# A two-layer hybrid RWKV/attention trunk on one core: the mixed-projection stage and the key-rate stage in one block, with key-rate block products inside a gate tile

## The chip, the cores and the metric

The kernel runs on one core of one Trainium2 chip. The metric is the device time of one execution in microseconds (us). PE is the matrix engine (TensorE), PEld its weight loads, DVE the vector engine, ACT the scalar engine, POOL the general-purpose engine (GpSimd), SP the engine that here only issues transfers. A wait in the profile is an engine's idle time with the instruction that ended it.

## The reference, cut to what matters

Two layers of a decoder trunk. Each layer multiplies the normalised residual stream h (1024 tokens and 16 meta tokens, 1024 channels) by one wide input matrix, whose columns feed an RWKV group, a latent-attention group and two gates:

```python
for l in range(DEPTH):
    p = h @ w_in[l]
    p_rwkv, p_mla, p_gate = jnp.split(p, [RWKV_COLS, RWKV_COLS + MLA_COLS], axis=-1)
    y_rwkv = _rwkv7_mix(p_rwkv, mu_shift[l], w0[l], w_lora_up[l], a0[l], a_lora_up[l], ...)
    y_mla = _mla(p_mla, pos, q_norm_g[l], w_uq[l], kv_norm_g[l], w_uk[l], w_uv[l])
    gate_rwkv, gate_mla = jnp.split(jax.nn.sigmoid(p_gate), N_BRANCHES, axis=-1)
    mixed = gate_rwkv * (y_rwkv @ w_proj_rwkv[l]) + gate_mla * (y_mla @ w_proj_mla[l])
    h = _layer_norm(DEEPNORM_ALPHA * h + mixed @ w_out[l], ln1_g[l], ln1_b[l])
    f = _conv_ffn(h, w_up[l], conv_w[l], conv_b[l], w_down[l])
    h = _layer_norm(DEEPNORM_ALPHA * h + f, ln2_g[l], ln2_b[l])
```

Inside `_rwkv7_mix` each column of p_rwkv is mixed with that of the token before (`p + (shift(p) - p) * mu`) and split into r, k, v and the low-rank inputs of decay and rate:

```python
w_raw = -jax.nn.softplus(-(w0 + jnp.tanh(wd) @ w_lora_up)) - 0.5
decay = jnp.exp(-jnp.exp(w_raw))
a = jax.nn.sigmoid(a0 + ad @ a_lora_up)
kk = kk / jnp.maximum(jnp.sqrt(jnp.sum(kk * kk, axis=-1, keepdims=True)), 1e-12)
k = k * (1.0 + (a - 1.0) * k_a)
```

The recurrence over tokens is computed in chunks of 104 tokens, for which the kernel prepares, per pair of heads, scaled copies of key, rate and query and the products of key and rate within each chunk.

## The kernel before, in words

Every stage is a `Phase`: one block with its own semaphores, which all engines leave through a barrier that also clears those semaphores. The change concerns two stages that follow each other in each of the two layers.

**The mixed-projection stage** (line 1433 on) forms 12 column tiles of 128 for r, k and v. A tile is `product` (line 226): for each of 8 slices k of the contraction, three passes (high by high, high by low, low by high halves of the fp32 numbers) of three 348-column matmuls, 72 in all, into one of two sets of three PSUM banks (`pset`). SP loads a 512 KB weight unit per tile, POOL splits it into its halves (lines 280 and 282), ACT copies the tile out (`raw0`/`raw1`, line 1551), DVE mixes neighbouring tokens (lines 1563 and 1565), ACT sends the result to HBM. Between its splits POOL forms sums of down-projection weights for a later stage (lines 1494 to 1500), with SP loading and storing them. At the end PE multiplies the first decay and rate products (`product32`, line 264, into both bank sets), then some matmuls that no one reads (`keep_warm`, line 257). SP has by then loaded the first mixed r, k, v and two units of gate weights, the first of which POOL splits (lines 287 and 289).

**The key-rate stage** (line 1638 on) works over four pairs of heads (j) and forms the 16 gate tiles G0 to G15 beside them. In the order of PE a pair is:

```python
pes.did(product32(one, [...]), f"zw{j}")          # decay, then za: rate; before j = 0 the stage before did both
pes.did(product32(one, [(head_ones[:, :], sqn[:, :])]), f"ss{j}")   # sums of squares
gate(g, two, ...); gate(g + 1, one, ...)          # two gate tiles
blocks(j, 0)                                      # key by rate, chunks 0 to 3
pes.did(product32(two, [(head_ones[:, :], rk[:, :])]), f"bn{j}")
blocks(j, 1)                                      # chunks 4 to 7
gate(g + 2, one, ...)
blocks(j, 2)                                      # chunks 8 and 9
```

`blocks` (line 1742) writes banks 6 and 7, and each part waits until ACT has copied the part before out of them (line 1799). For a pair ACT takes the sigmoids of decay and rate (lines 1814 and 1817), a logarithm and exponentials, the high halves of gate weights (`hi`, line 1782) and the gates' sigmoids (line 1788), after each of which it issues the store; DVE makes a running sum (line 1906), a maximum (line 1910), the low halves of gate weights (`lo`, line 1870) and the scaled copies up to `beta`, and beside the next pair it inverts 26 by 26 blocks of the pair before (lines 1876 and 1879). SP sends the copied-out blocks to HBM and back in the layout of that inversion (`pairs_out`, `blocks_in`), stores the inverses (line 1691) and loads weights. After the last pair, four gate tiles G12 to G15 remain, beside which the last inversion runs. The order on each engine is written out by hand as lists of step names; waits refer to these names.

An earlier stage already has a product with other matmuls within it: the hook `between` at line 1310 puts row sums (line 1288) ahead of slice k = 2 of a tile.

Of the kernel before, what the change touches and what calls it, by code (L numbers as in the profile page):

```python
# [18 lines left out]
ALU = mybir.AluOpType  # L19
# [134 lines left out]
def build(nc, a, out):  # L154
# [440 lines left out]
    def layer(l):  # L595
# [837 lines left out]
        with Phase(nc, "raw0_loaded", "raw1_loaded", "hi_done", "split", "used", "act_pre", "dve_pre",  # L1433
                   "act_steps", "dve_steps", "out0", "next_in",
                   "lora_in", "first0_in", "first1_in", "first_hi", "first_lo", "lora_up",
                   "wsum0_in", "wsum1_in", "wsum0_out", "wsum1_out", "wsum_steps") as (block, sm):
            loaded, hi_done, split, used = stream(sm[0:5])
            apre, dpre = Steps(sm[5], pre_act), Steps(sm[6], pre_dve)
            acts, dves = Steps(sm[7], ["raw0", "raw1"]), Steps(sm[8], ["mu0", "d0", "m0", "mu1", "d1", "m1"])
            outs = [Count(o, 1, 16) for o in (sm[9], rkv_landed[l])]  # L1440
            next_in = sm[10]
            lora_in, first_in, first_hi, first_lo, lora_up = sm[11], sm[12:14], sm[14], sm[15], sm[16]
            nt = 3 * RT
            wsum_in, wsum_out = sm[17:19], sm[19:21]
            sums = Steps(sm[21], [f"{n}{k}" for k in range(KF) for n in ("s1_", "s3_", "s2_", "s4_")])
            w_dn = a["w_down"][l]

            @block.sync
            def _(sp):
                def wsum_load(k):  # L1450
                    b = k % 2
                    if k >= 2:
                        sp.wait_ge(wsum_out[b], 16 * (k // 2))
                    for q, (kb, mb) in enumerate(((0, 1), (0, 0), (1, 1), (1, 0))):
                        sp.dma_start(wsum[b][:, q, :], w_dn[(kb * KF + k) * P:(kb * KF + k + 1) * P, mb * MF * P:(mb + 1) * MF * P]).then_inc(wsum_in[b], 16)

                def wsum_store(k):
                    sp.wait_ge(sums.sem, sums.of(0, f"s4_{k}"))
                    sp.dma_start(wsum_d[:, :, :, k, :].rearrange("q j p n -> p (q j) n"),
                                 wsum[k % 2][:, :, :].rearrange("p q (j n) -> p (q j) n", n=P)).then_inc(wsum_out[k % 2], 16)  # L1460
                split.give(sp)
                sp.sem_inc(split.sem, 2)
                for u in range(nt):
                    load_unit(sp, u + 2, u % 2, loaded, split, [(kview(KD), w_in_v[:, :, u * P:(u + 1) * P])])
                    if u in (0, 1):
                        wsum_load(u)
                    elif u >= 2:
                        wsum_store(u - 2)
                        if u < KF:
                            wsum_load(u)  # L1470
                wsum_store(KF - 1)
                sp.wait_ge(y_landed[l], 16 * (RT * NG // 2))
                sp.dma_start(w_l[0:DECAY_LORA, :], a["w_lora_up"][l, :, 0:P]).then_inc(lora_in, 16)
                sp.dma_start(w_l[DECAY_LORA:P, :], a["a_lora_up"][l, :, 0:P]).then_inc(lora_in, 16)
                sp.dma_start(reset[:, :], a["c_reset"]).then_inc(next_in, 16)
                sp.wait_ge(outs[0].sem, outs[0].of(RT + 1))
                for n in (1, 0, 2):
                    sp.dma_start(rkv[:, n, :], rkv_d[n * RT]).then_inc(next_in, 16)
                for s in range(2):
                    sp.wait_ge(split.sem, split.of(nt + s + 1))  # L1480
                    sp.dma_start(kview(KD)(w_raw[s]), w_in_v[:, :, GATE0 + s * P:GATE0 + (s + 1) * P]).then_inc(first_in[s], 16)
                sp.wait_ge(first_in[1], 16)
                for b in range(2):
                    sp.wait_ge(wsum_out[b], 16 * ((KF + 1 - b) // 2))
                sp.wait_ge(next_in, 16 * 4)

            @block.gpsimd
            def _(pool):
                def weight_sums(k):

                    b = k % 2
                    a11, a21, a12, a22 = (wsum[b][:, q, :] for q in range(4))
                    pool.wait_ge(wsum_in[b], 64 * (k // 2 + 1))
                    sums.did(nc.gpsimd.tensor_tensor(a22, a21, a22, ALU.add), f"s1_{k}")
                    pool.wait_ge(sums.sem, sums.of(0, f"s1_{k}"))
                    sums.did(nc.gpsimd.tensor_tensor(a21, a11, a21, ALU.subtract), f"s3_{k}")
                    pool.wait_ge(sums.sem, sums.of(0, f"s3_{k}"))
                    sums.did(nc.gpsimd.tensor_tensor(a11, a22, a11, ALU.subtract), f"s2_{k}")
                    pool.wait_ge(sums.sem, sums.of(0, f"s2_{k}"))
                    sums.did(nc.gpsimd.tensor_tensor(a12, a12, a11, ALU.subtract), f"s4_{k}")  # L1500
                used.give(pool)
                sums.give(pool)
                pool.sem_inc(hi_done.sem, 2)
                for u in range(nt):
                    split_unit(pool, u + 2, u % 2, u // 2 + 1, loaded, hi_done, split, (used.sem, used.of(u + 1)))
                    if u < KF:
                        weight_sums(u)
                pool.wait_ge(first_in[0], 16)
                pool.wait_ge(used.sem, used.of(nt + 1))
                split_next(pool, 0, first_hi, first_lo)  # L1510

            @block.tensor
            def _(pe):
                def tile(u, s):
                    pe.wait_ge(split.sem, split.of(u + 1))
                    product(pset[s], KD, wtile(w_hi[s], KD), wtile(w_lo[s], KD), hk(h_hi), hk(h_lo)).then_inc(used.sem, 1)
                pe.sem_inc(used.sem, 1)
                tile(1, 1)
                with pe.Fori(0, nt // 2) as i:
                    for s in range(2):  # L1520
                        pe.wait_ge(apre.sem, apre.of(0, ("raw_a", "raw_b")[s]))
                        pe.wait_ge(acts.sem, acts.of(i, f"raw{s}", 1))
                        tile(i * 2 + (2 + s), s)
                pe.wait_ge(lora_in, 32)
                pe.wait_ge(apre.sem, apre.of(0, "tanh"))
                for s in range(2):
                    rows = slice(s * DECAY_LORA, P if s else DECAY_LORA)
                    pe.wait_ge(acts.sem, acts.of(nt // 2 - 1, f"raw{s}"))
                    product32(pset[s], [(w_l[rows, :], lora_x[rows, :])]).then_inc(lora_up, 1)
                keep_warm(7, 3)  # L1530
                pe.wait_ge(lora_up, 2)

            @block.scalar
            def _(act):
                apre.give(act)
                acts.give(act)
                for s in range(2):
                    outs[s].give(act)
                for s in range(2):
                    act.wait_ge(used.sem, used.of(s + 1))  # L1540
                    act.wait_ge(dpre.sem, dpre.of(0, "pad1"))
                    apre.did(nc.scalar.activation(chunks3(raw_p[s][:, 1:TP + 1]), pset[s], ACT.Copy), ("raw_a", "raw_b")[s])
                act.wait_ge(dpre.sem, dpre.of(0, "m_c"))
                apre.did(nc.scalar.activation(lora_x[0:DECAY_LORA, :], lora_x[0:DECAY_LORA, :], ACT.Tanh), "tanh")
                apre.did(nc.scalar.activation(gd0[:, :], gd0[:, :], ACT.Sigmoid), "sg0")
                apre.did(nc.scalar.activation(gd1[ROPE:ROPE + G1, 1:TP + 1], gd1[ROPE:ROPE + G1, 1:TP + 1], ACT.Sigmoid), "sg1")
                with act.Fori(0, nt // 2) as i:
                    for s in range(2):
                        act.wait_ge(used.sem, used.of(i * 2 + (3 + s)))
                        act.wait_ge(dves.sem, dves.of(i, f"m{s}", 1))  # L1550
                        acts.did(nc.scalar.activation(chunks3(raw_p[s][:, 1:TP + 1]), pset[s], ACT.Copy), f"raw{s}")  # L1551
                        act.wait_ge(dves.sem, dves.of(i, f"m{s}"))
                        act.dma_start(rkv_d[i * 2 + s], mixed_p[s][:, :]).then_inc(outs[s].sem, 16)
# [28 lines left out]

        cursor[0] = gate_end
# [2443 lines left out]
```

## Time and profile before, and how to read it

| | us |
|---|---|
| three timed executions | 3688.88, 3690.66, 3691.11 |
| their median | 3690.66 |
| profiled execution, first to last instruction (span) | 3684.4 |
| PE busy in it | 3527.1 |
| DVE, POOL, ACT busy in it | 2374.1, 1538.0, 1316.6 |

For the profiled execution only its span is given, with no device time of its own; the median of the timed runs lies 6.26 us above the span. In the rows below a timeline line gives start and length in us, then engine, source line, operation, tiles written and read, the number of instructions merged, and in brackets the idle time before them with what ended it. "PEclk" is the granted clock of TensorE as a share of full speed.

### The profile page before, as it was taken

How to read it: one execution, taken by the hardware profiler on the slowest of the kernel's cores; microseconds unless marked ns; L12 is line 12 of the kernel's file. 1: busy time of each engine (PE TensorE's matmuls, PEld its weight loads, DVE VectorE, ACT ScalarE, POOL GpSimd, SP SyncE). 2: the span in 40 equal slices, each digit the busy share in tenths (PEclk: the TensorE clock that was granted, in tenths of full speed). 3: DMA queues.
4: the chain of work that ended last, by engine and by line, in shares of the span. 5: the costliest groups of instructions: out<-in, count | busy, mean ns of one | idle time of the engine just before them, and what ended most of it. 6: DMA issues, size and time to landing. Idle time of an engine off the chain costs nothing. (4 is left out here: it accounts for less than half of the span.)

```text
span 3684.4 us, 69094 instructions
## 1 busy us (share of the span) xinstructions
PE 3527.1 (96%) x29239; PEld 3297.9 (90%) x29239; DVE 2374.1 (64%) x2821; ACT 1316.6 (36%) x1900; POOL 1538.0 (42%) x875
## 2 busy tenths in 40 slices
PE   6999999999999999999999999999999999999998
PEld 6867988988898999999987689888889989999998
DVE  2374447665658877777835643585657597777687
ACT  5343124212213444453443520441231144444435
POOL 5364930000742655544444569000026435555341
PEclk9999999999999999999999999999999999999999
DMA  5521866422522222273334248563234122222732
GB/s 121 146 64 53 251 204 187 143 72 58 169 75 76 75 81 76 82 266 121 86 69 136 59 128 260 177 191 100 77 114 130 36 92 81 82 80 81 264 119 85
DMA packets 476187, 439.00 MB, mean 119 GB/s; under 512 B 106027, under 2 KB 401159, under 8 KB 475895
## 3 DMA queue, kind: packets, MB, share of 16 engines
q1 hardware_dynamic: 455640, 383.02, 34.5%
q10 hardware_dynamic: 20255, 51.78, 3.8%
q8 instruction: 221, 3.62, 0.4%
q14 instruction: 71, 0.58, 0.0%
HBM read 297.14 MB, written 137.05 MB: 118 GB/s over the span
## 5 line engine op out<-in xcount | busy, mean ns | idle before, releaser
L234 PE MATMUL psum<-h_hi,w_hi 128*128 128x348 f32 x1632 | 355.3, 326 | 10.7 <-ACT lat_sq L864 3.7
L234 PE MATMUL psum<-h_lo,w_hi 128*128 128x348 f32 x1632 | 348.7, 322 | 0.0
L234 PE MATMUL psum<-h_hi,w_lo 128*128 128x348 f32 x1632 | 347.6, 321 | 0.0
L234 PEld LDWEIGHTS psum<-h_hi,w_hi 128*128 128x128 f32 x1632 | 274.7, 189 | 19.6 <-POOL w_lo L282 4.3
L234 PEld LDWEIGHTS psum<-h_lo,w_hi 128*128 128x128 f32 x1632 | 277.3, 189 | 0.0
L234 PEld LDWEIGHTS psum<-h_hi,w_lo 128*128 128x128 f32 x1632 | 274.9, 188 | 0.0
L3255 POOL TENSOR_TENSOR piece_lo_w<-sum,piece_hi_w 128x512 fp32r<-128x512 f32 x120 | 209.5, 1746 | 141.6 <-ACT piece_hi_w L3557 138.5
L3300 PE MATMUL psum<-t_hi,piece_hi_w 128*128 128x260 f32 x1280 | 258.2, 283 | 5.1 <-issue 2.6
L3300 PE MATMUL psum<-t_hi,piece_lo_w 128*128 128x260 f32 x1280 | 257.3, 282 | 0.0
L3300 PE MATMUL psum<-t_lo,piece_hi_w 128*128 128x260 f32 x1280 | 257.2, 282 | 0.0
L280 POOL TENSOR_TENSOR w_hi<-w_raw,consts 128x1024 fp32r<-128x1024 f32 (+1 forms) x78 | 126.9, 1627 | 295.5 <-PE psum L234 108.8
L2032 POOL TENSOR_TENSOR g<-gd,g_hi 32x1044 fp32r<-32x1044 f32 x2 | 4.8, 2390 | 535.3 <-ACT g_hi L2210 535.3
L3300 PEld LDWEIGHTS psum<-t_hi,piece_hi_w 128*128 128x128 f32 x1280 | 197.7, 188 | 6.3 <-DVE t_lo L3843 3.3
L3300 PE MATMUL psum<-h_hi,piece_hi_w 128*128 128x260 f32 x960 | 194.0, 283 | 6.3 <-DVE uv_second L3879 5.3
L3300 PEld LDWEIGHTS psum<-t_lo,piece_hi_w 128*128 128x128 f32 x1280 | 197.4, 188 | 0.0
L3300 PEld LDWEIGHTS psum<-t_hi,piece_lo_w 128*128 128x128 f32 x1280 | 196.7, 188 | 0.0
L3300 PE MATMUL psum<-h_hi,piece_lo_w 128*128 128x260 f32 x960 | 194.1, 283 | 0.0
L3300 PE MATMUL psum<-h_lo,piece_hi_w 128*128 128x260 f32 x960 | 193.7, 283 | 0.0
L3255 POOL TENSOR_TENSOR piece_lo_w<-raw_g,piece_hi_w 128x512 fp32r<-128x512 f32 x80 | 123.8, 1547 | 157.3 <-ACT piece_hi_w L3557 157.3
L282 POOL TENSOR_TENSOR w_lo<-w_raw,w_hi 128x1024 fp32r<-128x1024 f32 (+1 forms) x78 | 175.6, 2251 | 6.1
L1563 DVE TENSOR_TENSOR diff<-raw_p 128x1044 f32<-128x1044 f32 x28 | 52.4, 1871 | 184.7 <-ACT raw_p L1551 164.6
L3807 DVE SCALAR_TENSOR_TENSOR cg_row<-ug_row,vecs,cg_row 128x1040 f32<-128x1040 f32 x80 | 130.7, 1634 | 50.6 <-ACT cg_row L3503 50.6
(655 smaller groups left out, 9749.7 us busy)
## 6 DMA issues: line engine op xcount, KB each, us to landing
w_raw<-in_w_in SPq DMA_DIRECT2D x68, 512.0 KB, 8.8
wsum<-in_w_down SPq DMA_DIRECT2D x88, 256.0 KB
wsum_scratch<-wsum SPq DMA_DIRECT2D x22, 1024.0 KB
raw_g<-in_w_up SPq DMA_DIRECT2D x40, 512.0 KB, 3.8
raw_v<-in_w_up SPq DMA_DIRECT2D x40, 512.0 KB, 3.9
gate_scratch<-gst ACTq DMA_DIRECT2D x32, 522.0 KB, 3.0
gbuf<-gate_scratch SPq DMA_DIRECT2D x32, 522.0 KB, 3.6
prep_scratch<-prep ACTq DMA_DIRECT2D x8, 2080.0 KB, 8.3
```

Of the source, the lines that this page charges most:

```text
L234: last = nc.tensor.matmul(bank[:, n, :], w(k), x(k)[:, nrange(n)], start=(k == 0 and q == 0), stop=(k == kt - 1 and q == 2))
L280: nc.gpsimd.tensor_tensor(w_hi[s][:, 0:width], w_raw[s][:, 0:width], consts[:, 4:5].broadcast_to([P, width]), ALU.mult).then_inc(hi_done.s ...
L282: nc.gpsimd.tensor_tensor(w_lo[s][:, 0:width], w_raw[s][:, 0:width], w_hi[s][:, 0:width], ALU.subtract).then_inc(split.sem, 1)
L1563: me.did(nc.vector.tensor_tensor(d[rows, :], raw[rows, 0:TP], raw[rows, 1:TP + 1], ALU.subtract), names[0])
L2032: nc.gpsimd.tensor_tensor(g96[G1R, 1:TP + 1], gd1[G1R, 1:TP + 1], g0_hi[G1R, :], ALU.subtract).then_inc(gate_low, 1)
L3255: w_los.did(nc.gpsimd.tensor_tensor(piece_lo_w[:, q, :], weight_piece[q], piece_hi_w[:, q, :], ALU.subtract), f"{q}_{p}")
L3300: last = nc.tensor.matmul(psum[:, bank + c, 0:TQ], w, x_(k)[:, c * TQ:(c + 1) * TQ], start=(not more and k == 0 and n == 0), stop=(k == MF ...
L3807: dves.did(stt(c, t[:, n:T + n], vecs[:, at + 2 * n * FT:at + 2 * n * FT + 1], c, ALU.mult, ALU.add), f"t{n}{x_}{p}")
```

## The change

The two stages become one block: one set of semaphores, and no barrier between them. The first gate weights are loaded and split as a thirteenth unit of the first stage, so that G0 follows the last r, k, v tile directly. The first decay product, sum of squares and rate product are put into G0 ahead of slices 1, 3 and 5. So each pair now has the gate tiles g + 1, g + 2 and g + 3 in place of g, g + 1 and g + 2, and three tiles (G13 to G15) remain after the last pair. Parts two and three of a pair's blocks are put into tile g + 3, ahead of its slices 2 and 5. The other engines' orders follow: ACT and DVE take the first pair's steps in the order in which G0 needs them, loads and splits of gate weights come one unit earlier, and ACT copies the third part of the blocks out before the sigmoid of the tile that now holds it. The `keep_warm` matmuls between the stages go. The diff, cut to its core (moved code left out):

```diff
-        with Phase(nc, "raw0_loaded", "raw1_loaded", "hi_done", "split", "used", "act_pre", "dve_pre",
-                   "act_steps", "dve_steps", "out0", "next_in",
...
+        with Phase(nc, "raw0_loaded", "raw1_loaded", "hi_done", "split", "used", "act_pre", "dve_pre",
+                   "r_act_steps", "r_dve_steps", "out0", "lora_in",
...
             @block.sync
...
+                load_unit(sp, nt + 2, 0, loaded, split, [(kview(KD), w_in_v[:, :, GATE0:GATE0 + P])])
+                wsum_store(KF - 1)
...
+                for u in (1, 2):
+                    sp.wait_ge(split.sem, split.of(nt + 1 + u))
+                    sp.dma_start(kview(KD)(w_raw[u % 2]), w_in_v[:, :, GATE0 + u * P:GATE0 + (u + 1) * P]).then_inc(raw_in[u % 2].sem, 16)
...
             @block.gpsimd
...
-                split_next(pool, 0, first_hi, first_lo)
+                split_unit(pool, nt + 2, 0, nt // 2 + 1, loaded, hi_done, split, (used.sem, used.of(nt + 1)))
...
             @block.tensor
...
-                keep_warm(7, 3)
-                pe.wait_ge(lora_up, 2)
...
+                def first_rows(k):
+                    if k == 1:
+                        pe.wait_ge(lora_in, 32)
+                        pe.wait_ge(apre.sem, apre.of(0, "tanh"))
+                        pe.wait_ge(racts.sem, racts.of(nt // 2 - 1, "raw1"))
+                        pes.did(product32(pset[1], [(w_l[0:DECAY_LORA, :], lora_x[0:DECAY_LORA, :])]), "zw0")
+                    if k == 3:
+                        pe.wait_ge(acts.sem, acts.of(0, "sq0"))
+                        pes.did(product32(pset[1], [(head_ones[:, :], sqn[:, :])]), "ss0")
+                    if k == 5:
+                        pe.wait_ge(dves.sem, dves.of(0, "ssm0"))
+                        pes.did(product32(pset[1], [(w_l[DECAY_LORA:P, :], lora_x[DECAY_LORA:P, :])]), "za0")
+                pe.wait_ge(split.sem, split.of(nt + 3))
+                pe.wait_ge(racts.sem, racts.of(nt // 2 - 1, "raw0"))
+                pes.did(product(pset[0], KD, wtile(w_hi[0], KD), wtile(w_lo[0], KD), hk(h_hi), hk(h_lo), first_rows), "G0")
...
-                    gate(g, two, (acts.sem, acts.of(0, f"a{j}")))
-                    gate(g + 1, one, (dves.sem, dves.of(0, f"ssm{j}")))
+                    gate(g + 1, two, (acts.sem, acts.of(0, f"a{j}")))
+                    gate(g + 2, one, (dves.sem, dves.of(0, f"ssm{j}")) if j else (acts.sem, acts.of(0, "g0")))
                     blocks(j, 0)
-                    pe.wait_ge(acts.sem, acts.of(0, f"g{g}"))
+                    pe.wait_ge(acts.sem, acts.of(0, f"g{g + 1}"))
                     pe.wait_ge(dves.sem, dves.of(0, f"rk{j}"))
                     pes.did(product32(two, [(head_ones[:, :], rk[:, :])]), f"bn{j}")
-                    blocks(j, 1)
-                    gate(g + 2, one, (acts.sem, acts.of(0, f"g{g + 1}")))
-                    blocks(j, 2)
+                    def later_blocks(k, j=j):
+                        if k in (2, 5):
+                            blocks(j, 1 if k == 2 else 2)
+                    gate(g + 3, one, (acts.sem, acts.of(0, f"g{g + 2}")), later_blocks)
...
             @block.scalar
...
-                square(0)
+                hi(1)
...
+                    act.wait_ge(pes.sem, pes.of(0, f"zw{j}"))
+                    acts.did(nc.scalar.activation(chunks3(sw[:, :]), one if j else two, ACT.Sigmoid, bias=vcol(V_W0, j)), f"sw{j}")
+                    if j == 0:
+                        mixed_out(nt // 2 - 1, 1)
+                        square(0)
+                        wsum_landed(act)
+                        hi(2)
...
                     if j + 1 < RT:
                         square(j + 1)
-                    gate(g + 2, one)
                     blocks(j, 2)
+                    gate(g + 3, one)
...
             @block.vector
...
+                lo(1)
                 dve.wait_ge(reset_in, 16)
                 dve.wait_ge(mid_pad, 1)
+                dve.wait_ge(rdves.sem, rdves.of(nt // 2 - 1, "m1"))
...
+                    if j == 0:
+                        lo(2)
                     dve.wait_ge(pes.sem, pes.of(0, f"ss{j}"))
...
-                    lo(g + 2)
                     lo(g + 3)
+                    lo(g + 4)
```

Between the sigmoid of zw0 and the square, ACT issues the store of the last mixed tile (`mixed_out`), which waits for DVE's `m1` of that tile; `wsum_landed` waits for the last store of the weight sums, whose memory later tiles reuse.

## Rows read from the trace of the kernel before

**Rows 1.** The page, busy time of the engines over the whole span.
```profile
PE 3527.1 (96%) x29239; PEld 3297.9 (90%) x29239; DVE 2374.1 (64%) x2821; ACT 1316.6 (36%) x1900; POOL 1538.0 (42%) x875
```

**Rows 2.** Waits of PE over the whole span: us in total, times, longest.
```profile
PE psum L264 <- ACT sw L1814: 12.5, 8, 5.8
...
PE psum L1742 <- ACT adg L1799: 6.9, 8, 1.6
```

**Rows 3.** Timeline of PE where the two stages meet, layer 0.
```profile
504.78 3.30 PE L264 MATMUL psum<-lora_x,w_l 64*128 64x348 f32 x12
...
516.20 3.85 PE L264 MATMUL psum<-sqn,head_ones 128*128 128x348 f32 x6 [5.84 <-ACT sw L1814]
519.33 1.59 PE L234 MATMUL psum<-h_hi,w_hi 128*128 128x348 f32 x3
...
521.45 0.64 PE L234 MATMUL psum<-h_hi,w_lo 128*128 128x348 f32 x3
```

**Rows 4.** Windows, same place: us, busy of PE, PEld, DVE, ACT, POOL, PEclk, DMA.
```profile
516.20:519.33 3.13, 3.13 (x7) 1.92 (x7) 2.50 (x2) 2.25 (x2) 0.00 (x0) 0.50 0.45 134
```

**Rows 5.** Timeline of PE where the two stages meet, layer 1.
```profile
2312.89 3.30 PE L264 MATMUL psum<-lora_x,w_l 64*128 64x348 f32 x12
...
2325.34 1.58 PE L234 MATMUL psum<-h_hi,w_hi 128*128 128x348 f32 x3
...
2327.30 0.64 PE L234 MATMUL psum<-h_hi,w_lo 128*128 128x348 f32 x3
```

**Rows 6.** Timeline of ACT, sigmoid of the last gate tile of layer 0.
```profile
740.63 1.04 ACT L1788 ACTIVATE gst<-psum 128x1044 f32<-128x1044 f32 x1 [10.41 <-PE psum L234]
```

**Rows 7.** Timeline of PE, row sums inside a product, an earlier stage.
```profile
341.97 0.63 PE L234 MATMUL psum<-h_hi,w_lo 128*128 128x348 f32 x3
342.53 0.68 PE L1288 MATMUL psum<-racc,ones 128*64 128x272 f32 x4
...
343.73 0.63 PE L234 MATMUL psum<-h_lo,w_hi 128*128 128x348 f32 x3
```

**Rows 8.** Timeline of PE around one pair of heads, layer 0.
```profile
559.62 0.61 PE L1742 MATMUL psum<-prep 64*104 64x104 f32 x8
560.07 2.77 PE L264 MATMUL psum<-lora_x,w_l 64*128 64x348 f32 x12
563.23 2.02 PE L264 MATMUL psum<-sqn,head_ones 128*128 128x348 f32 x6 [0.39 <-ACT sw L1814]
564.83 0.90 PE L234 MATMUL psum<-h_hi,w_hi 128*128 128x348 f32 x3
565.56 0.64 PE L234 MATMUL psum<-h_lo,w_hi 128*128 128x348 f32 x3
...
588.99 2.02 PE L264 MATMUL psum<-rk,head_ones 128*128 128x348 f32 x6
592.21 0.98 PE L1742 MATMUL psum<-prep 64*104 64x104 f32 x16 [1.20 <-ACT adg L1799]
593.12 0.74 PE L234 MATMUL psum<-h_hi,w_hi 128*128 128x348 f32 x3
```

**Rows 9.** Timeline of ACT, POOL and DVE where the stages meet, layer 0.
```profile
505.91 1.89 POOL L287 TENSOR_TENSOR w_hi<-w_raw,consts 128x1024 fp32r<-128x1024 f32 x1 [12.82 <-DMA w_raw<-in_w_in]
...
508.94 3.27 DVE L1565 SCALAR_TENSOR_TENSOR mixed_p<-diff,mu,raw_p 128x1044 f32<-128x1044 f32 x1
...
515.03 1.11 ACT L1814 ACTIVATE sw<-psum,vecs 128x1044 f32<-128x1044 f32 x1
...
516.28 2.33 DVE L1906 TENSOR_TENSOR_SCAN cum<-reset,sw 128x1040 f32<-128x1040 f32 x1 [2.25 <-ACT sw L1814]
...
520.08 1.25 DVE L1910 TENSOR_SCALAR sqn<-psum 128x1044 f32<-128x1044 f32 x1 [1.27 <-PE psum L264]
```

**Rows 10.** Timeline of SP and PE at the end of the key-rate stage, layer 0.
```profile
728.45 3.02 SPq L1691 DMA_DIRECT2D inverse_scratch<-tit  x4
...
740.43 1.56 PE L257 MATMUL psum<-pair_mask,ident 104*104 104x416 f32 x4
```

More of the change, by code:

```diff
@@ L1638, in layer @@
-        dve_n += [f"lo{g + 2}"] + solve_names(RT - 1, 0) + [f"lo{g + 3}"] + solve_names(RT - 1, 1)
-        with Phase(nc, "raw0_loaded", "raw1_loaded", "pe_steps", "act_steps", "dve_steps",
+            pe_n += [f"zw{j}", f"za{j}", f"ss{j}"] if j else ["zw0", "ss0", "za0", "G0"]
+            pe_n += [f"G{g + 1}", f"G{g + 2}", f"P{j}_0", f"bn{j}", f"P{j}_1", f"P{j}_2", f"G{g + 3}"]
+            act_n += [f"sw{j}", f"a{j}"] if j else ["hi1", "sw0", "sq0", "hi2", "a0"]
+            act_n += [f"ln{j}", f"rn{j}"] + [f"{n}{j}" for n in ("eA", "eR", "eB", "eK", "eD")] + ([] if j else ["g0"])
@@ new lines, in layer @@
+            lora_in = sm[10]
+            nt = 3 * RT
+            wsum_in, wsum_out = sm[11:13], sm[13:15]
+            sums = Steps(sm[15], [f"{n}{k}" for k in range(KF) for n in ("s1_", "s3_", "s2_", "s4_")])
+            w_dn = a["w_down"][l]
+            raw_in = [Count(s, 0, 16) for s in sm[16:18]]
+            pes, acts, dves = Steps(sm[18], pe_n), Steps(sm[19], act_n), Steps(sm[20], dve_n)
+            rkv_in, w_got, reset_in = sm[21:24]
+            bonus_out, prep_out = Count(sm[24], 0, 16), Count(sm[25], 0, 16)
@@ L1723, in _, with tile @@
             @block.tensor
             def _(pe):
-                pes.give(pe)
-                def gate(u, bank, free):
-                    if u >= 1:
-                        pe.wait_ge(dves.sem, dves.of(0, f"lo{u}"))
+                def tile(u, s):
+                    pe.wait_ge(split.sem, split.of(u + 1))
+                    product(pset[s], KD, wtile(w_hi[s], KD), wtile(w_lo[s], KD), hk(h_hi), hk(h_lo)).then_inc(used.sem, 1)
+                pe.sem_inc(used.sem, 1)
+                tile(1, 1)
@@ new lines, in _ @@
+                with pe.Fori(0, nt // 2) as i:
+                    for s in range(2):
+                        pe.wait_ge(apre.sem, apre.of(0, ("raw_a", "raw_b")[s]))
+                        pe.wait_ge(racts.sem, racts.of(i, f"raw{s}", 1))
+                        tile(i * 2 + (2 + s), s)
+                pes.give(pe)
+                def first_rows(k):
[10 more added lines that the diff above has]
+                        pes.did(product32(pset[1], [(w_l[DECAY_LORA:P, :], lora_x[DECAY_LORA:P, :])]), "za0")
@@ L1832, in _ @@
                     acts.did(nc.scalar.activation(decay[:, j, :], dsum[:, :], ACT.Exp, scale=-DECAY_C), f"eD{j}")
-                    hi(g + 2)
-                    gate(g, two)
+                    if j == 0:
+                        gate(0, one)
                     hi(g + 3)
+                    gate(g + 1, two)
+                    hi(g + 4)
                     act.wait_ge(dves.sem, dves.of(0, f"beta{j}"))
@@ L1838, in _ @@
                                   prep[:, :, :, :].rearrange("p c q n -> p c (q n)")).then_inc(prep_out.sem, 16)
-                    gate(g + 1, one)
-                    hi(g + 4)
+                    gate(g + 2, one)
+                    hi(g + 5)
                     blocks(j, 0)
```

333 lines of the change are left out of this document (143 added, 190 removed).

## The prediction

> **What bounds the kernel now.** I read the page first: PE is busy for 96% of the span and no other engine for two thirds of it [rows 1], so a change pays only where PE waits, runs slowly or does useless work. The list of waits names the two places that the change touches: PE before the sums of squares, waiting for ACT's decay sigmoid (8 times, 12.5 us, one of them 5.8), and PE before the key-rate blocks, waiting for ACT to empty their banks (8 times, 6.9 us) [rows 2]. Then the timeline where the stages meet. In layer 0 the last r, k, v tile ends at 504.78, where the first decay and rate products start; then come the matmuls that no one reads, 5.84 us of nothing, the sums of squares at 516.20 and G0 at 519.33 [rows 3]. The granted clock, 1.00 while the tiles run, is 0.50 in that last stretch, the lower level of 1.2 GHz [rows 4]: the sums of squares take 3.85 us where a later pair takes 2.02 [rows 3, 8], and the first two passes of G0 take 2.12 us (519.33 to 521.45). In layer 1 the same stretch goes from 2312.89 to 2325.34 and 2327.30 [rows 5].
>
> **Units.** ACT waits 10.41 and works 1.04 between two gate tiles at the end of the stage, so a tile with nothing in it takes 11.45 us [rows 6]: 1.43 for each of its 8 slices, 0.477 for each of its 24 passes. What putting something into a tile costs is seen in an earlier stage: without the row sums the pass at 343.73 would start two passes after 341.97, at 342.92. The insertion cost 0.81 us for 0.68 us of matmuls, so 0.13 beyond its own busy time [rows 7]. I take 0.13 for each insertion, from the only place where this kernel does it. The bounds are 0 and, since what follows a sum of squares also starts with a slow pass (0.73 in place of 0.477, [rows 8]), 0.38.
>
> **Part 1, the meeting of the stages.** Before, from the end of the last tile to the end of G0: 504.78 to 521.45, then 22 passes of 0.477, so 27.2 us in layer 0, and by the same sum 24.9 in layer 1. That is 52.1 in all. After: one tile (11.45), both decay and rate products (2.77), the sums of squares (2.02 at full clock) and three insertions (0.39): 16.6 us a layer, if nothing waits. The gap of 5.84 goes, and with it the reason for the lower clock, since PE never stops.
>
> Does anything wait? I count from the end of the last tile. PE is through slice 0 at 1.43; ACT has emptied the tile's banks at about 1.25 (the 1.04 of such a pass and its start), so zw0 can go: PE until 2.95. ACT meanwhile makes the high halves of unit 1 (to 2.3), takes the sigmoid (2.95 to 4.1, 1.11 in [rows 9]), issues the store of the last mixed tile (DVE's two passes at 1.25 each are done by about 3.9), then squares (to about 5.6). PE is through slices 1 and 2 at 5.8: the sums of squares wait for nothing, or for a tenth or two. They end at 7.95. DVE: low halves of unit 1 to 5.1, running sum 2.33 to 7.5, low halves of unit 2 to 8.7, maximum 1.25 to 10.0 [rows 9]; PE wants it at slice 5, at 10.8. The rest is looser: G2 needs G0's sigmoid, behind a logarithm and exponentials on ACT, some 3 us before PE asks.
>
> What lies ahead of this chain on other queues: unit 1 of the gate weights must be in SBUF at 1.25. Before, the first gate unit, issued at the same point of SP's queue, had landed when POOL took it up at 505.91, that is at 1.13 [rows 9]. SP issues one unit more before the weight sums' last store, but one less later, so the transfers in that queue are the same; POOL splits the extra unit right after tile 12, a whole tile (11.45) ahead of G0, and its first half takes 1.89 [rows 9]. The DVE pass that took 3.27 us while POOL was splitting [rows 9] should be back at 1.25, since POOL has nothing left then. I allow 0.3 us of waiting per layer: 16.9 after, so 52.1 - 33.8 = **18.3 us** saved in both layers.
>
> **Part 2, the blocks inside the third tile.** Before, around one pair: from the sums bn (588.99) to the tile after part two (593.12) 4.13 us, with 1.20 of waiting, 0.10 for that tile's slow first pass (0.74 where 0.64 is usual), and 0.45 for part three ahead of zw (559.62 to 560.07): 4.68. After: from bn to the tile directly, as from the sums of squares to theirs (563.23 to 564.83, 1.60, and 0.25 of slow first pass), part two 0.98 + 0.13, part three 0.61 + 0.13: 3.70 [rows 8]. So 0.98 is saved where 1.20 was waited, 0.22 less than the wait. The 8 waits average 0.86 [rows 2]: 8 x 0.64 = **5.1 us**. ACT has 2 slices (2.9 us) after bn to empty the banks, of which it needs some 1.2, then three slices more, so no new wait stands there. Between 0 (insertions at the upper bound use it up) and 6.9.
>
> **What moves and costs nothing.** za of the next pair now waits for the sigmoid of the tile just finished, in the same banks. ACT needs 1.04 and PE spends half of 2.77 on zw meanwhile: covered by about 0.2 us, and if that cover fails, by tenths. ACT squares the next pair's keys ahead of emptying part three; the keys are asked for right after bn, and part three is multiplied five slices and part two later (8.2 us), so only a transfer of more than some 7 us would make that late, and ACT alone. SP sends the blocks out earlier. At the end of the stage three whole tiles and three slices follow the last part, in place of four tiles: 7.2 us less cover for the last inversion. Before, its last store was issued by 731.47, 9.0 us ahead of the last tile's end at 740.43 [rows 10]; ACT now empties part three without a sigmoid ahead of it (1.04), so some 2.8 remain for the landing. Just covered; past it, each microsecond is lost.
>
> **The sum.** 18.3 + 5.1 = 23.4 us. The traced span of 3684.4 is 6.26 below the median of the runs; what lies around the span is untouched, so I subtract from the median: 3690.66 - 23.4 = **3667.3 us**. A difference of under 0.2% (7.4 us) can't be told from none.
>
> **Rivals.**
>
> *The chain within G0 runs late.* DVE, ACT and a transfer must keep a pace that was hidden before by an idle PE; the margins are 0 to 0.8 us. For it: the unit in SBUF only 0.1 us ahead, and orders in which high halves stand ahead of the sigmoid. Against it: the same transfers had landed in time. Each microsecond late costs one per layer; late by 3 gives back 6: 3673. At worst the old wait of 5.84 returns twice: 3679.
>
> *The last inversion ends the stage.* If the stores land 5 us late in both layers, 10 are given back: 3677. For it the margin of 2.8; against it, nothing else is left in that queue.
>
> *The insertions break PE's pace: slower than before.* PE would lose its clock in tiles that hop between banks. Five tiles a layer hold insertions. At 1.2 GHz a tile takes 11.45 us more; with half of each of the ten tiles at that level 57 us are lost: 3725. It decides from 2.3 us a tile, 1.6 slices at the lower level. Against it: after the one insertion that I can see, passes go on at full pace, and tiles change bank with every matmul as it is; the clock fell only after 5.84 us of idleness.
> The Trainium skill, "TensorE: Matmul & The Clock Gate", section "A second HAM failure mode: psum-queue depth-cycling", speaks for this rival: cycling through PSUM banks can leave short idle gaps in which the clock gate swings between its levels, and throughput falls. By that rule the time would be this rival's; the trace so far does not agree, with 0.477 us a pass in tiles that cycle three banks.
>
> *The change does not do what it says.* If the meeting point merely moves the wait (G0's weights split late, say, because POOL is also busy with weight sums), little but part 2 is left: about 3686. POOL's last sums end one tile and more before; small.
>
> **How the numbers follow.** Forecast 0.68, around 3667 (3662 to 3671); late chain 0.14; inversion 0.07; no real effect 0.07; slower 0.04. The low end takes no waits in G0 (0.6) and insertions at 0 (22 x 0.13 = 2.9): 3663.8, or 3662 if part 2 gives all of its 6.9. The high end takes insertions at 0.38 (11 a layer, 5.5) and half of a late chain: 3677. Faster by over 0.2% needs 3683.3 or less: 0.68 + 0.14 + 0.07 less the worst of these two, 0.88. Within 0.2%: 0.08; slower: 0.04.
>
> **What would show it.** Right: G0's first pass within 0.2 us of the last tile's end; no idle of PE above a few tenths until the first pair's blocks; granted clock 1.00 throughout; the decay product after 3 passes, the sums of squares after 9; no wait of PE for the emptied banks in the list; part three 4.3 us ahead of the tile's end; the stage's barrier right after the last sigmoid. Wrong: PE idle ahead of the sums of squares or the rate product in G0, with ACT or a transfer as releaser; a wait of SP for inverse stores after the last tile; passes of tiles with insertions above 0.5 us.

## The result, and the profile after

Four executions of the changed kernel took 3656.03 to 3671.33 us, median 3660.07; four of the kernel before, 3690.89. The ratio is 0.992 [0.9901, 0.994]: faster by 0.8%, 30.8 us where 23.4 were forecast. The forecast ratio, 3667.3 / 3690.66 = 0.9937, lies within that interval, but the median of 3660.07 lies below the low end of the range, 3662.

The traced execution spans 3660.2 us, 24.2 less than that of before. PE's busy time is the same to 0.7 us [rows 1]; what went is time in which PE stood. Page, busy time of the engines:

```profile
PE 3526.4 (96%) x29227; PEld 3297.2 (90%) x29227; DVE 2374.8 (65%) x2821; ACT 1315.9 (36%) x1900; POOL 1539.3 (42%) x875
```

Waits of PE over the whole span (us in total, times, longest); both waits of [rows 2] are gone from the list, and the wait for POOL's halves, also in the list before, is now among the largest of this part of the program:

```profile
PE psum L528 <- DVE tok L434: 13.5, 1, 13.5
PE psum L1256 <- ACT q_hi L1331: 7.9, 18, 0.6
PE psum L264 <- ACT grs L3454: 5.5, 2, 2.9
...
PE psum L234 <- POOL w_lo L282: 3.8, 6, 1.5
```

Where the stages meet in layer 0 (timeline of PE; compare [rows 3]), G0's first pass at 501.77 follows the last tile without a gap. No row of the window has a bracket, so PE never stood:

```profile
501.77 0.65 PE L234 MATMUL psum<-h_hi,w_hi 128*128 128x348 f32 x3
...
503.30 2.02 PE L264 MATMUL psum<-lora_x,w_l 64*128 64x348 f32 x6
505.25 0.74 PE L234 MATMUL psum<-h_hi,w_hi 128*128 128x348 f32 x3
505.83 0.64 PE L234 MATMUL psum<-h_lo,w_hi 128*128 128x348 f32 x3
506.31 0.63 PE L234 MATMUL psum<-h_hi,w_lo 128*128 128x348 f32 x3
...
508.21 1.92 PE L264 MATMUL psum<-sqn,head_ones 128*128 128x348 f32 x6
509.70 0.90 PE L234 MATMUL psum<-h_hi,w_hi 128*128 128x348 f32 x3
...
512.35 0.64 PE L234 MATMUL psum<-h_hi,w_lo 128*128 128x348 f32 x3
512.92 2.02 PE L264 MATMUL psum<-lora_x,w_l 64*128 64x348 f32 x6
514.87 0.74 PE L234 MATMUL psum<-h_hi,w_hi 128*128 128x348 f32 x3
```

Windows of the same place, G0, then G1 with G2, then all from the last r, k, v tile to the next stage (us; busy of PE, PEld, DVE, ACT, POOL; PEclk; DMA share; GB/s). PE is busy throughout G0 to G2, and the granted clock is 1.00 in all three, where [rows 4] show 0.50:

```profile
501.77:519.34 17.57, 17.57 (x93) 14.71 (x92) 13.99 (x14) 9.55 (x9) 0.00 (x0) 1.00 0.37 107
519.34:542.24 22.90, 22.90 (x145) 22.68 (x144) 9.80 (x9) 10.99 (x12) 0.00 (x0) 1.00 0.46 166
501.77:728.10 226.33, 224.94 (x1414) 208.34 (x1413) 151.66 (x295) 95.80 (x108) 0.00 (x0) 1.00 0.53 166
```

Around a pair (timeline of PE; compare [rows 8]) parts two and three stand between passes of one tile:

```profile
547.96 0.98 PE L1684 MATMUL psum<-prep 64*104 64x104 f32 x16
548.87 0.74 PE L234 MATMUL psum<-h_hi,w_hi 128*128 128x348 f32 x3
...
553.35 0.61 PE L1684 MATMUL psum<-prep 64*104 64x104 f32 x8
553.89 0.73 PE L234 MATMUL psum<-h_hi,w_hi 128*128 128x348 f32 x3
...
558.37 3.22 PE L264 MATMUL psum<-lora_x,w_l 64*128 64x348 f32 x12
561.61 2.02 PE L264 MATMUL psum<-sqn,head_ones 128*128 128x348 f32 x6
```

End of the stage, timelines of SP and of PE (compare [rows 10]):

```profile
720.39 3.02 SPq L1587 DMA_DIRECT2D inverse_scratch<-tit  x4
728.03 8.44 SPq L2023 DMA_DIRECT2D xc<-inverse_scratch  x16
```

```profile
725.21 1.56 PE L257 MATMUL psum<-pair_mask,ident 104*104 104x416 f32 x4
728.10 0.60 PE L2074 MATMUL psum<-pc 64*104 64x208 f32 x4 [1.33 <-SPq L2010]
```

**Where the 24.2 us came from.** I cut each trace at four points: the end of the last r, k, v tile (504.78 before; 501.77 after) and the first product of the next stage (743.23; 728.10), in both layers. The two stretches in between hold everything the change touches. In the first layer the stretch went from 238.45 to 226.33, in the second from 236.74 to 226.33: 22.5 us. The other 1.7 lie in stages whose code is the same.

Each stretch splits at part one of pair 0 (543.49 before, 542.24 after, with G0, G1 and with G0, G1, G2 ahead of it) and at the end of the last tile:

| us saved | layer 0 | layer 1 | sum | forecast |
|---|---|---|---|---|
| meeting: to part one, less G1 or less G1 and G2 at 11.45 each | 27.26 - 17.57 = 9.7 | 24.97 - 17.57 = 7.4 | 17.1 | 18.3 |
| pairs: part one of pair 0 to the end of the last tile | 2.5 | 3.1 | 5.6 | 5.1 |
| end of the stage | -0.1 | -0.1 | -0.2 | 0 |

### The profile page after: what moved, and what is told of

Read it like the earlier page. It is cut to its first block and busy times, and to the rows that moved or that the text cites. A ratio compares the mean times of both kernels' runs of the same rounds, so it can differ in the third digit from the quotient of the medians.

```text
span 3660.2 us, 68992 instructions
## 1 busy us (share of the span) xinstructions
PE 3526.4 (96%) x29227; PEld 3297.2 (90%) x29227; DVE 2374.8 (65%) x2821; ACT 1315.9 (36%) x1900; POOL 1539.3 (42%) x875
```

## The experiments

Nine experiments ran, three of them repeats without an edit. "Stretch" is the one just defined; the rest is the span less both stretches. Clock is the mean granted clock over the timed runs, where the list of runs gives it.

| kernel | ratio to before | stretches, layers 0 and 1 | rest of the traced span | clock |
|---|---|---|---|---|
| before | | 238.45, 236.74 | 3209.2 | |
| before again | 0.9996 [0.9986, 1.0006] | 238.45, 237.60 | 3209.2 | 0.9888 (51 runs) |
| changed | 0.992 [0.9901, 0.994] | 226.33, 226.33 | 3207.5 | 0.9914 (16 runs, all three) |
| changed, again | 0.9926 [0.9909, 0.9944] | 226.38, 226.37 | 3211.9 | |
| changed, third | 0.9924 [0.991, 0.9939] | 226.38, 226.37 | 3214.2 | |
| merge only | 0.9954 [0.994, 0.9968] | 231.87, 231.17 | 3217.3 | 0.9898 |
| parts only | 0.9984 [0.9974, 0.9995] | 233.98, 234.21 | 3224.0 | 0.9881 |
| rows first | 0.9973 [0.9964, 0.9983] | 234.75, 234.95 | 3216.8 | 0.9887 |
| near parts | 0.9928 [0.9912, 0.9943] | 226.40, 226.39 | 3211.4 | 0.9912 |
| rows near | 0.9929 [0.9912, 0.9946] | 227.89, 227.88 | 3207.6 | 0.9915 |
| warm meeting | 1.0003 [0.9991, 1.0015] | 239.45, 240.92 | 3208.5 | 0.9903 |

The stretches are a sharper measure than the runs: in the three traces of the changed kernel they agree to 0.05 us, while the rest, which no edit touched, differs by 16.5 us over the eleven traces.

### The changed kernel again, and a third time

No edit.

> The changed kernel, nothing else altered. The two traces put 12.2 us (first layer) and 10.5 us (second) of the gain between the end of the last r,k,v tile and the end of the stage, 22.7 in all, while the medians of the timed runs stood 30.8 apart. Theory A (the stage gains what was forecast, and the other 7 to 8 us are differences between executions in stages that the change doesn't touch): in a new trace the two stretches take 223 to 224 us again, within 0.5, and the median of new runs lies anywhere from 22 to 31 below the kernel before. Theory B (the stage gains more in most executions than in the one traced): the two stretches come out 3 us or more shorter than 223.4, with the median again about 30 below.

> The changed kernel a third time. Two traces give 226.3 and 226.4 us for each of the four stretches from the end of the last r,k,v tile to the first product of the next stage, against 238.5 and 236.7 before: 22.5 us, within 0.1 in each trace. In the untouched rest the times differ by up to 17 us from execution to execution, with the stretches in which the clock stands at half. Theory A (22.5 in the stretches is the whole effect; the distance of the medians beyond it is the spread of the rest): stretches of 226.3 to 226.4 again, a median between 3660 and 3672, and at the same mean clock (0.990) an execution 20 to 23 us under one of the kernel before. Theory B (the change also makes the rest faster by 4 to 8 us, through fewer stretches at half clock elsewhere): again a mean clock of 0.991 to 0.993 over the runs where the kernel before has 0.988 to 0.989, and a median of 3664 or less.

Medians 3664.59 (3655.18 to 3670.08, 6 runs) and 3660.36 (3657.98 to 3668.64, 6 runs) against 3689.72 (22 runs) and 3690.34 (17 runs): 25.1 and 30.0 us. The stretches are the same as in the first trace, so the touched stages gain 22.5 and no more, and theory B of the first expectation fails. (The first expectation measures to the end of the last tile, 223.4; the stretch here goes 2.9 further, to the next stage's first product.) Of the two theories of the second expectation neither is excluded: the stretches, the median and the mean clock (0.9914 over all runs against 0.9888) fit both. Compared at the same mean clock, the distance is 20 us (0.990: median 3666.4 of 5 runs, against 3686.2 of 14) or 24 us (0.991: 3662.0 of 5, against 3685.9 of 4). So the touched stages gain what the traces show, and what the medians show beyond it goes with a higher clock over the run.

### The kernel before, again

No edit.

> The kernel before, for a second trace and its mean clock over the runs. The stretch from the last r,k,v tile to the next stage's first product comes out between 236 and 239 us in each layer (its meeting holds a stretch at half clock whose place may move by a microsecond or two). The time outside the span is 2.1 us as in every timed run, so that the execution traced first (span 3684.4) was one of about 3686.5 us, 4 us under the median of the runs. If instead 4 us or more lie outside the span of the traced execution, the distance between span and median was not a matter of which execution was traced.

Median 3688.2 (12 runs). The traced execution took 3687.31 with a span of 3685.2: 2.1 us lie outside the span. In the changed kernel it is 1.8 (3662.03 and 3660.2). Over all runs it is 1.7 to 1.9 in the kernels with one block and 2.1 to 2.2 in those with two. The execution traced first (span 3684.4) was therefore one of about 3686.5 us. Against this second trace the changed kernel's stretches save 23.4.

### Merge only

```diff
-                    gate(g + 3, one, (acts.sem, acts.of(0, f"g{g + 2}")), later_blocks)
+                    blocks(j, 1)
+                    gate(g + 3, one, (acts.sem, acts.of(0, f"g{g + 2}")))
+                    blocks(j, 2)
```

with ACT's order put back to match.

> One block and G0 with its three insertions as in the changed kernel; parts two and three of each pair stand outside the gate tile as in the kernel before. By the sum of the forecast (18.3 for the meeting, 5.1 for the pairs) this is 5.1 slower than the changed kernel: each stretch from the last r,k,v tile to the end of the stage takes 226.0 instead of 223.4, and the wait of part two on the eviction of part one is back at about 0.86 x8. Rival (the pairs gain nothing, since what the insertions cost eats the wait): same time as the changed kernel within 1 us. Rival (the meeting gains little by itself): 15 us or more slower than the changed kernel.

Each stretch is 5.5 and 4.8 us longer than in the changed kernel: 10.3, twice what was expected. Up to the end of the last tile 2.5 and 1.7 of it appear: these are the waits of the pairs, back in the list and about as forecast. The other 6 us come at the end of the stage. Waits of PE, the first row twice 4.4 where the changed kernel has 1.3:

```profile
PE psum L2073 <- SPq L2009: 8.8, 2, 4.4
...
PE psum L1684 <- ACT adg L1771: 5.4, 8, 1.2
...
PE psum L264 <- ACT sw L1785: 2.3, 6, 0.4
```

Timelines of SP and PE at that end:

```profile
730.17 3.32 SPq L1587 DMA_DIRECT2D inverse_scratch<-tit  x4
736.31 7.93 SPq L2022 DMA_DIRECT2D xc<-inverse_scratch  x16
```

```profile
730.44 1.56 PE L257 MATMUL psum<-pair_mask,ident 104*104 104x416 f32 x4
736.38 1.03 PE L2073 MATMUL psum<-pc 64*104 64x208 f32 x4 [4.38 <-SPq L2009]
```

The last inverse stores are issued by 733.49 and SP goes on 2.82 later: here the last inversion ends the stage. With part three of the last pair behind tile g + 3, and no longer with four tiles to come, the inversion starts too late. So the two parts of the change are not independent. Taking over a tile from the first pair shortens the cover of the last inversion, and moving part three into the tile gives most of it back.

### Parts only

The edit of merge only the other way round, on the kernel before: two blocks, with parts two and three ahead of slices 2 and 5 of tile g + 2.

> The kernel before with its two blocks, with parts two and three of each pair inside the third gate tile. By the sum of the forecast 5.1 us faster than the kernel before (each stage 2.5 shorter than the 233.9 to 235.7 before), the wait on the eviction of part one gone, the wait for the decay sigmoid (12.5 over 8) untouched. Rival (insertions eat the wait): within 1 us of the kernel before.

Ratio 0.9984 [0.9974, 0.9995], 3.7 us between the medians. From part one of pair 0 to the end of the last tile it takes 194.63 in both layers, where before took 196.94 and 197.53: 5.2 saved, against 5.1 expected. (The whole stretches differ by 7.0, because the meeting also varies from trace to trace: PE's wait there was 5.84 and 4.37 in the first trace, 5.17 and 4.62 in the second.) The wait on the emptied banks is gone. Of the 8 waits for the decay sigmoid two are left, those of the meeting; the expectation had called all 8 untouched. Waits of PE:

```profile
PE psum L264 <- ACT sw L1816: 9.3, 2, 4.8
```

### Rows first

```diff
-                pes.did(product(pset[0], ..., first_rows), "G0")
+                pes.did(product(pset[0], ...), "G0")
```

with the calls `first_rows(1)`, `(3)` and `(5)` ahead of G0.

> The changed kernel with the three small products of pair 0 (zw, ss, za) ahead of G0 in place of inside it: the block is still one, but PE stands through the chain. From the trace of the changed kernel: waits of about 1.5 (eviction of the last tile), 2.3 (decay sigmoid and square) and 1.9 (maximum) us, so 5.7 per layer less the three insertions' own overhead of about 0.35 each: 4.6 per layer, 9 us in all slower than the changed kernel, if hiding the chain inside G0 is worth what its waits show. If the clock falls over the chain as it did before the change (0.50 in one stretch), 1 to 3 us per layer more. If nearly all of the 18 us came from the barrier and the reload between the blocks and not from the chain, less than 3 us slower.

17.0 us are given back, not 9: 8.4 and 8.6 per layer. That leaves 5.5 of the 22.5, which is what parts two and three bring by themselves. One block without the chain inside G0 is worth nothing. Timeline of PE, then the window behind the second wait:

```profile
512.83 2.08 PE L264 MATMUL psum<-lora_x,w_l 64*128 64x348 f32 x6 [1.22 <-ACT raw_p L1739]
517.18 3.85 PE L264 MATMUL psum<-sqn,head_ones 128*128 128x348 f32 x6 [2.27 <-ACT sqn L1781]
522.37 2.02 PE L264 MATMUL psum<-lora_x,w_l 64*128 64x348 f32 x6 [1.34 <-DVE sqn L1914]
```

```profile
517.00:519.00 2.00, 1.82 (x3) 1.18 (x4) 1.97 (x3) 1.07 (x2) 0.00 (x0) 0.50 0.85 204
```

The brackets are 4.83 per layer, near the 5.7 expected. The rest is the clock: after the stands it is 0.50, and the sums of squares take 3.85 in place of 1.92.

### Near parts

```diff
-                        if k in (2, 5):
+                        if k in (2, 3):
```

> The changed kernel with part three of each pair one slice (1.43 us) after part two in place of three slices after it. The eviction of a part takes two activations of 0.66 us or so each and showed a wait of 0.6 to 1.6 us where 2.0 us of other work stood between. If the spacing is what removed that wait: a wait of 0.5 to 1.3 us is back at part three of each of 8 pairs, 4 to 10 us in all, so that each stage stretch grows from 226.3 to 228.5 to 231. If one slice is enough: within 0.3 us of 226.3, and the gain came from the insertion as such.

The stretches are 226.40 and 226.39, the same as in the changed kernel, so one slice is enough, and the expectation was wrong about the cause. Timeline of PE:

```profile
548.14 0.98 PE L1684 MATMUL psum<-prep 64*104 64x104 f32 x16
...
550.66 0.61 PE L1684 MATMUL psum<-prep 64*104 64x104 f32 x8
```

Between the two parts PE has 1.6 us of work, no more than the sums bn gave before, and yet no wait. The timeline of ACT in the kernel before, around part one (543.49), shows why it was different there:

```profile
543.60 1.04 ACT L1788 ACTIVATE gst<-psum 128x1044 f32<-128x1044 f32 x1 [8.87 <-PE psum L234]
...
545.15 1.06 ACT L1782 ACTIVATE w_hi<-w_raw 128x1024 fp32r<-128x1024 f32 x1 [0.51 <-DMA w_raw<-in_w_in]
546.11 0.91 ACT L1799 ACTIVATE adg<-psum 104x416 f32<-104x416 f32 x2
```

Copying a part out takes 0.91 us, but ACT first had the sigmoid of the tile just finished and a high half to do. The wait was for ACT's queue at a tile's end. In the middle of a tile that queue is empty.

Part of that queue is itself a wait, for the weights of a later gate tile: the bracket ahead of the high half. In the kernel before it is 0.46 or 0.47 where PE waits 0.60, and it is 0.47 in the changed kernel too, where the row names no transfer. Around the second pair of layer 0 it is longer, and PE's wait there, 1.20 [rows 8], is longer by the same 0.6 (timeline of ACT, kernel before):

```profile
590.29 1.06 ACT L1782 ACTIVATE w_hi<-w_raw 128x1024 fp32r<-128x1024 f32 x1 [1.07 <-DMA w_raw<-in_w_in]
```

So of the 6.9 us in eight waits, 4.8 (0.60 each) are the queue, and 2.1 are gate weights that had not landed.

### Rows near

```diff
-                    if k == 3:
+                    if k == 2:
...
-                    if k == 5:
+                    if k == 3:
```

> The changed kernel with the insertions of pair 0 ahead of slices 1, 2 and 3 of G0 in place of 1, 3 and 5. By the trace the squares are done 5.78 us and the maximum 9.74 us after the end of the last tile; ahead of slice 2 PE stands at 4.9 and ahead of slice 3 at about 8.9. So waits of 0.9 and 0.9 us are expected, 1.8 per layer and 3.6 in all, each stretch 228.1 in place of 226.3. If these short waits also bring the clock down in the stage, 1.5 to 3 us more per layer. If the chain is faster than the stamps say (no waits), 226.3.

Timeline of PE, layer 0:

```profile
511.06 2.02 PE L264 MATMUL psum<-sqn,head_ones 128*128 128x348 f32 x6 [0.65 <-ACT sqn L1779]
...
515.04 2.02 PE L264 MATMUL psum<-lora_x,w_l 64*128 64x348 f32 x6 [0.53 <-DVE sqn L1912]
```

Waits of 0.65 and 0.53 where 0.9 and 0.9 were expected, and stretches longer by 1.5. The chain runs at the pace the stamps showed, slices 3 and 5 give it what it needs, and waits as short as these did not bring the clock down.

### Warm meeting

On the kernel before, at the end of the r, k, v block:

```diff
-                keep_warm(7, 3)
+                keep_warm(7, 7)
```

> The kernel before with seven dummy products in place of three at the end of the r,k,v block (5.5 us in place of 2.3), so that PE stands 2.7 us in place of 5.8 (first layer) and 1.3 in place of 4.4 (second) at the meeting; nothing waits less. If the clock at the meeting falls because PE stands still there: the product ss of pair 0 runs at full clock (2.0 us in place of 3.85 and 3.2), the granted clock of the stretch behind it stays above 0.9, the two stage stretches shrink from 238.5 and 236.7 by 2 to 4 us each, and the mean clock of the runs rises by about 0.0014 over the 0.9888 of the kernel before. If the clock's fall has nothing to do with the length of the stand: 238 again. If clearing the meeting of half clock also spares half clock in stages behind it (what would explain 4 us by which the runs of the changed kernel gain more than the stretches): a mean clock of 0.991 or more, and a time 8 us or more under the kernel before.

Timeline of PE, layer 0, and the window behind it:

```profile
506.02 5.14 PE L257 MATMUL psum<-pair_mask,ident 104*104 104x416 f32 x14
514.36 3.62 PE L264 MATMUL psum<-sqn,head_ones 128*128 128x348 f32 x6 [3.21 <-ACT sw L1814]
```

```profile
515.00:520.00 5.00, 5.00 (x20) 3.76 (x19) 3.92 (x4) 2.31 (x3) 0.00 (x0) 0.70 0.14 40
```

It failed as a test of the clock: PE still stood for 3.21 us in both layers, where 2.7 and 1.3 were expected, and the clock still fell. The stretches are 1.0 and 4.2 longer. From the end of the last tile to part one of pair 0 both layers take 38.1 us, against 38.7 and 36.4 before, so the longer row of dummy products held up the meeting in the second layer alone. The rest lies behind it, with the waits on emptied banks, 4.8 us in each layer against 3.2 and 3.7, and in the second layer with a lower clock after the first of them (part two of pair 0 takes 1.64 us there in place of 0.98). In pair 0 of the first layer the gate weights landed late (timelines of ACT and PE):

```profile
544.06 1.06 ACT L1782 ACTIVATE w_hi<-w_raw 128x1024 fp32r<-128x1024 f32 x1 [2.01 <-DMA w_raw<-in_w_in]
545.98 0.98 PE L1742 MATMUL psum<-prep 64*104 64x104 f32 x16 [2.15 <-ACT adg L1799]
```

It does show a floor for this order: even when PE comes to the barrier late, it stands 3.2 us until ACT has squared and taken the sigmoid. Whether a meeting at full clock would make later stages faster stays open. The mean clock over the runs was 0.9903, against 0.9891 in the 17 runs of the kernel before beside them, and no time was gained.

## Why the prediction was right, and where it was wrong

**The direction and the places were right.** Waits for the emptied banks and for the decay sigmoid left the list, PE stands for no more than 0.1 us from the last r, k, v tile to the barrier at the end of the stage, the clock is 1.00 there, and part three ends 4.5 us ahead of its tile's end (4.3 forecast).

**Part 1: 17.1 against 18.3.** The before side was right (27.26 and 24.97, forecast 27.2 and 24.9). The after side is 17.57 per layer, forecast 16.9. Nothing waits, so the 0.3 allowed for that was not used; the insertions cost more. From the pass ahead of an insertion to the one behind, less a pass of 0.477, and with the slow first pass after it, zw0 and za0 take 2.1 each and ss0 1.8. The forecast had 1.39 + 0.13 for each of the first two and 2.02 + 0.13 for the third. The 1.39 was half of a pair of products that ran behind another small product [rows 8]; directly behind a tile the same pair takes 3.24 (558.37 to 561.61) in place of 2.77, and one of the two alone takes 1.95 to the next pass (503.30 to 505.25), more than half of either. That is the term of this part that was mis-sized. A row of the kernel before pointed to it: in [rows 3] the pair stands directly behind a tile, and takes 3.30.

The chain's times were right to a few tenths. Counted from the end of the last tile, the squares are done at 5.78 (forecast 5.6), the sums of squares end at 7.93 (7.95) and the maximum is done at 9.74 (10.0). PE asks for it at 11.15 (10.8).

**Part 2: 5.6 against 5.1,** 5.2 when done alone. The insertions cost 1.1 for part two and 0.7 for part three, as forecast (1.11 and 0.74). The reading of the wait was incomplete: it counted how long ACT needs to empty the banks, while most of it was ACT's queue ahead of that (near parts). And that the sum is met so closely is partly luck. It books 0.45 per pair for taking part three from ahead of zw, but the pair of products, now directly behind the tile, grew by 0.47; and the wait of 0.39 for the decay sigmoid, which the sum left alone, went away. The two nearly cancel in the six places where a pair follows.

**The last inversion** is "just covered", as forecast. Its last store was issued by 723.41, 1.8 us ahead of the last tile's end where 2.8 were forecast. The 2.82 us that merge only shows from the last store to SP's next transfer hold the landing and then the barrier. The barrier alone takes 1.26 in the changed kernel, from the end of PE's last dummy product at 726.77 to SP's next transfer at 728.03. So the landing takes some 1.6 us, an estimate, and is done at about 725.0, before those dummy products end. In merge only this rival came true and cost 3 us per layer.

**The late chain** did not happen; rows near prices it.

**The insertions do not break PE's pace.** Passes between insertions still follow at 0.477 (505.83, 506.31, 506.78) and the granted clock is 1.00 in tiles with insertions. The Trainium skill, "TensorE: Matmul & The Clock Gate", section "A second HAM failure mode: psum-queue depth-cycling", tells of a kernel that cycles through PSUM banks, in which PE idles briefly between groups of matmuls and the clock swings. The trace shows neither here, with no idle of PE and 1.00 over the 17.57 us of G0.

**What failed is the step from the sum to the time and its range: whatever lies outside the two stages was put at nothing.** Of the 30.8 us between the medians the stretches hold 22.5; the other 8.3 lie elsewhere. "The traced span of 3684.4 is 6.26 below the median of the runs; what lies around the span is untouched, so I subtract from the median." Only 2.1 us lie around the span (1.8 in the changed kernel, so this too is not quite untouched); the other 4.2 were the traced execution's own, one of the quicker ones. And the range (3662 to 3677) was built from the bounds of the costs alone, as if executions agreed. They don't: the rest of the span, the same code, takes 3207.5 to 3224.0 in eleven traces, and the changed kernel ran between 3655 and 3671. A median of a few such runs moves by some microseconds: 3660.07, 3664.59 and 3660.36 for the same kernel. The sum itself held: it forecast 23.4 for the stretches, which measured 22.5 and, against the second trace of before, 23.4.

**What stays open.** Over all jobs the changed kernel's medians lie 25 to 31 us below, some 4 us more than its stretches give. It goes with the mean clock, 0.0026 higher. The half clock that left the meeting, whose gain the stretches already hold, explains half of that clock or somewhat more: in the first trace 3.5 and 1.7 us of clock were lost there (length times what is missing of 1.00), 0.0014 of the span, and in the second 0.0018. The remainder would lie in stages that were not edited, but no trace shows it: the rest of the changed kernel's three traced executions (3207.5, 3211.9, 3214.2) is not shorter than that of before (3209.2 twice). All three took longer than the median of their runs, and none of the quick ones was traced. So the cause of these 4 us stays open.

## What to carry to other kernels

Merging two blocks pays by what can be put into the stand between them: the chain of small dependent products inside a full tile brought 17 us, the merged block without it nothing. Before moving work later in a stage, find what its last consumer is (here the inversion behind part three), because the cover at the end is shared by both edits. And when a change is worth less than 1%, compare the touched stretch in the traces and give the predicted time the width by which executions of the same code differ.

## What the hardware showed that was not expected

**The same stand may or may not bring the clock down.** At one place of an unedited stage PE stands 1.37 or 1.38 us for DVE, in every trace. In merge only (timeline, then windows) the clock is then 0.50 for ten microseconds and more:

```profile
1988.63 0.29 PE L1241 MATMUL psum<-ident_r,nm 128*35 128x128 f32 x1 [1.38 <-DVE nm L1370]
```

```profile
1990.00:1995.00 5.00, 5.00 (x18) 3.86 (x15) 0.64 (x1) 0.98 (x2) 0.00 (x0) 0.50 0.91 222
1995.00:2000.00 5.00, 5.00 (x20) 4.37 (x20) 3.14 (x4) 0.98 (x2) 1.81 (x1) 0.50 0.00 0
```

In the first trace of the kernel before it stays at 1.00:

```profile
1988.21 0.22 PE L1241 MATMUL psum<-ident_r,nm 128*35 128x128 f32 x1 [1.38 <-DVE nm L1370]
```

```profile
1988.00:1993.00 5.00, 4.79 (x28) 3.92 (x29) 1.64 (x3) 2.41 (x5) 0.00 (x0) 1.00 1.15 278
1993.00:1998.00 5.00, 4.99 (x30) 3.39 (x29) 3.74 (x4) 1.51 (x4) 2.53 (x2) 1.00 0.03 8
```

The rest of a span goes with the sum of such stretches. Clock lost there, taken from windows of 5 us, is 27 to 38 us in the eight traces whose rest is 3207.5 to 3214.2, 38 and 44 us in those with 3216.8 and 3217.3, and 52 us in the one with 3224.0. So much of the spread between executions seems to be how many stands happened to end at the lower level; no run sets this apart from other causes.

**What stands ahead of a small product changes its time.** The same pair of decay and rate products took 3.24 us directly behind a tile and 2.77 behind a block product, both at a clock of 1.00. Part three ahead of the pair therefore cost next to nothing: from the start of the tile's last pass to the end of the pair it was 3.79 us with it (559.05 to 562.84, kernel before) and 3.81 without it (557.80 to 561.61, changed kernel).
